# Sums of squares in the heads and around the embedding: high and low halves, multiplied with ones in the rounded format

## The chip, the cores and the metric

The kernel runs on one core of a Trainium2 chip. TensorE (PE) multiplies 128x128 tiles, VectorE (DVE), ScalarE (ACT) and GpSimd (POOL) work elementwise, and SyncE (SP) issues most of the DMAs. The metric is the device time of one execution in microseconds; a lower one is better.

## The reference

A sequence of 512 tokens of width 1024 goes through three layers in float32: a layer with differential attention, a short convolution and a gated embedding; a layer with a Fourier mixer and a SwiGLU; and a layer with four retention heads and a SwiGLU. What matters here are the root-mean-square norms:

```
attn = rms_norm(attn, subln_gain[i], SUBLN_EPS) * (1.0 - lambda_init)     # per attention head, 128 features
x = x + rms_norm(mixed, post_norm_gain[i])                                # "post", 1024 features
e = rms_norm(p[i] @ w_ple_proj[i], ple_norm_gain[i])                      # "ple", the embedding
x = x + jax.nn.sigmoid(x @ w_ple_gate[i]) * e
...
y = (y - mu) * lax.rsqrt(var + EPS)                                       # per retention head, 512 features
```

## The kernel before

Everything is held with features on the 128 partitions and tokens along the row (512), so the sum of squares over features of a norm crosses partitions. It is made in two steps. ACT squares the tiles of 128x512 and DVE adds them into `sqsum`; then PE multiplies `sqsum` with a 128x128 matrix of ones, which sums over partitions and spreads the result to all of them (`stats`, L1765). ACT takes logarithm and exponential of it (`rsqrt`, L439) and leaves `rinv`.

Weights stream from HBM in chunks of 8 tiles of 128x128 (512 KB). SP loads a chunk into `w_raw` (L325), ACT rounds it to `w_hi` in float32r (L430), POOL subtracts and leaves the rest in `w_lo` (L399, four pieces a chunk), and PE makes each product of three multiplications, `w_lo` with the rounded activations, `w_hi` with their rest, and `w_hi` with the rounded ones (`mul`, L1610: rows L1614, L1617, L1618). A group below means these three. Each buffer of a chunk comes free when PE has used it. The multiplications with ones alone are in plain float32: `ones` and `sqsum` are float32 tensors.

Each engine runs its instructions in the order in which the code writes them, and semaphores tie the engines together. The order around the norms:

- **Attention heads** (a loop of four turns; the last turn's tail runs in the gemm of `w_out`). PE multiplies the softmax weights with the values (`values`, L1836), then goes on with groups of the next gemm; after the tenth of them (`body_tail`, n == 9) it waits for `o_sq` and does `stats`, after the fifteenth (n == 14) it turns `ada_acc` with eight transposes (`ada_turn`, L1795). ACT copies and squares the attention output (L581, L582) and then copies the convolution output (L584), rounds a chunk and waits for the sum. DVE in between finishes the convolution (L1194) and does three steps of `ada` (L891, a chunk of ADA times a scalar, added to `ada_acc`): one, then the rest of the convolution output, then two. `ada_raw` has two buffers, so SP issues the load for one step when the step before last has run. After these steps DVE makes the head's output (L1207 on).
- **After the heads** ACT loads the embedding's input through its own queue (L593), rounds it (L595), and only then rounds the chunks of the `out` gemm from its fifth on.
- **"post"** (`norm_stats`, L1776). Seven of the eight squares are in `sqsum`; the eighth is multiplied with ones apart, from `sq`, and both products add up in the bank. It stands after tile m == 1 of the embedding's gemm (`gemm_e`). `rinv` then starts DVE's chain L1245, L1246, L1239, which makes X and its low part for the gate gemm, eight times.
- **"ple"** is the same in the gate gemm, after group n == 27. Its `rinv` starts DVE's chain of eight embedding tiles (L1263) and eight gate tiles (L1289, L1290, L1275, L1283), and its end lets PE form the next norm's columns (`rinv_columns`, L1939, row L1943).
- **Retention heads**. The squares of four tiles are added by DVE (`add_sq`, L1508); PE multiplies them after group n == 4 of the tile t + 10 (`group_stats`, L2102). Then come `product`, `normed`, `gate` and `y_low` on DVE, with ACT's `gate` and `y_high` between them. The last head's `y_low(3)` (L1531) is needed soon after by the gemm of `w_ret_out`.

Of the kernel before, what the change touches and what calls it, by code (L numbers as in the profile page):

```python
# [16 lines left out]
P = 128  # L17
# [122 lines left out]
def build(nc, W, ADA, XT, PT, COLS, DIST, ROPE, DECAY, OUT):  # L140
# [3 lines left out]
    with ctx:  # L144
# [25 lines left out]
        ones = sb("ones", [P, P])  # L170
# [82 lines left out]
        zc_t, cv_out = sem("zc_t"), sem("cv_out")  # L253
        p_hi, p_ready = sem("p_hi"), sem("p_ready")
# [35 lines left out]
        def added(v):  # L290

            return 6 * (v - (v > 3))
# [127 lines left out]
        def _(act):  # L420
# [136 lines left out]
            with act.Fori(0, NH) as i:  # L557
# [24 lines left out]
                act.activation(sqsum[:, :], banks[:, 4, :], ACT.Square).then_inc(o_sq, 1)  # L582
                act.wait_ge(cv_out, at("one", 1))
# [22 lines left out]

            def e_tile(m):
                t = TI["ple"] + m
                wait_tile(act, flat, t)
                read_out(act.activation(E[:, m, :], banks[:, BANK[t], :], ACT.Copy), t)  # L610
# [5 lines left out]
            e_tile(0)  # L616
            e_tile(1)
# [37 lines left out]
            for n in range(8):  # L655
                if n not in (3, 7):
                    split_w(flat, c0 + n + 4)
                if n == 1:
# [115 lines left out]
            def head(at, c, t):  # L774
# [44 lines left out]
                for n in range(3):  # L819
                    y_high(n)  # L820
# [47 lines left out]
        def _(dve):  # L868
# [47 lines left out]
            def add_square(v, m):  # L916

                if m in (-1, 0, KD - 1):
                    return
# [137 lines left out]
            dve.memset(ones[:, :], 1.0).then_inc(const, 1)  # L1057
# [86 lines left out]
            with dve.Fori(0, NH) as i:  # L1144
# [49 lines left out]
                dve.tensor_tensor(tmp[:, 0, :], tmp[:, 0, :], sq[:, 1, :], ALU.mult).then_inc(cv_out, 1)  # L1194
                ada(at, 1)
# [40 lines left out]

            def xg_lo(m):
# [15 lines left out]
            for m in range(KD):  # L1253
                add_square(2, m)

# [218 lines left out]
            def head(at, t):  # L1474
# [44 lines left out]
                add_sq(3)  # L1519

# [71 lines left out]
        def _(pe):  # L1592
# [43 lines left out]
            def split_tiles(v, t0, ks, rhs, ready, mid):  # L1636
# [15 lines left out]
                for m in SPLIT[v]:  # L1652
                    out = banks[:, BANK[t0 + m], BACK]
                    wait_bank(flat, t0 + m)
                    for n, k in enumerate(ks):
# [3 lines left out]
                        if count == mid:  # L1659
                            pe.wait_ge(half_sum, SPLIT_AT[v] + len(SPLIT[v]))  # L1660
                            pe.matmul(aux[:, FRONT], ones[:, :], sqsum[:, FRONT], start=True,
# [7 lines left out]
            def back_stats(v):  # L1669
                pe.wait_ge(full_sum, v - 3)  # L1670
                pe.wait_ge(half_ln, v - 3)
                pe.matmul(aux[:, BACK], ones[:, :], sqsum[:, BACK], start=True, stop=True).then_inc(aux_ready, 1)
# [92 lines left out]
            def stats(at, u):  # L1765
# [3 lines left out]
                pe.matmul(aux, ones[:, :], sqsum[:, :], start=True, stop=True).then_inc(aux_ready, 1)  # L1769

            def keep_warm(n=1):

                for _ in range(n):
                    pe.matmul(banks[:, 6, :], ones[:, :], cols[:, 0:S], start=True, stop=True)

            def norm_stats(v, name):  # L1776

                pe.wait_ge(sq_added, added(v) + 6)
                if AUX[name] > 0:
                    pe.wait_ge(aux_free, AUX[name])  # L1780
                pe.matmul(aux, ones[:, :], sqsum[:, :], start=True, stop=False)
                pe.wait_ge(sq_ready, 8 * v + 8)
                pe.matmul(aux, ones[:, :], sq[:, 1, :], start=False, stop=True).then_inc(aux_ready, 1)
                if name not in ("post", "ple", "final"):
                    keep_warm(2 if name == "four" else 1)
# [19 lines left out]
            for _ in range(WARM):  # L1805
                pe.matmul(banks[:, 6, 0:P], ones[:, :], ones[:, :], start=True, stop=True)
# [58 lines left out]
            def body_tail(at, n):  # L1865
# [49 lines left out]
            def gemm_e(t0):  # L1915

                for m in range(KD):
# [3 lines left out]
                    if m == 1:  # L1921
                        norm_stats(1, "post")
# [7 lines left out]
            def gate_hook(n):  # L1930
                if n == 27:
                    norm_stats(2, "ple")
# [169 lines left out]
            def group_stats(at):  # L2102

                pe.wait_ge(y_qs, at("three", 3))
                stats(at, AUX["ret"])
# [168 lines left out]
```

## Time and profile before

| | us |
|---|---|
| median of 3 runs | 1576.48 |
| lowest and highest of them | 1573.29, 1576.93 |
| the profiled execution | 1575.09 |
| its span | 1573.1 |
| PE busy in it | 1551.9 (99%) |
| DVE, ACT, POOL busy | 810.0, 594.5, 871.9 |

The span is the time between the first and the last instruction of the profiled execution, 2.0 us less than its own time. The granted clock of PE was full in all 40 slices of the span. A row of a timeline gives the start and the time taken in us, engine, line, operation and tiles, and, in brackets, how long the engine had been idle and what ended that. Ends of PE rows are modelled: the start of the next row tells what a multiplication took from its neighbours.

### The profile page before, as it was taken

To read this page: it belongs to the slowest core of one execution; us is meant where nothing else is said; L and a number is where in the kernel's file an instruction comes from. 1 tells how busy PE (TensorE), PEld (TensorE's weight loads), DVE (VectorE), ACT (ScalarE), POOL (GpSimd) and SP (SyncE) were. 2 spreads that over 40 slices of the span, in tenths; PEclk is the share of its full clock that TensorE was granted. 3 is DMA by queue.
4 is the path that set the end of the run, shared out by engine and by line. 5 is a ranking of instruction groups with operands and counts; after the bars stand their busy time and mean duration, and the time that the engine had idled before them with its cause. 6 is when DMAs were issued, how large, how long until landed. Compare 5 with 4: busy or idle time off the path is not lost.

```text
span 1573.1 us, 21372 instructions
## 1 busy us (share of the span) xinstructions
PE 1551.9 (99%) x7316; PEld 1286.8 (82%) x7316; DVE 810.0 (51%) x1131; ACT 594.5 (38%) x873; POOL 871.9 (55%) x1040
## 2 busy tenths in 40 slices
PE   8999999999999999999999999999999999999997
PEld 7777778898888888888888888888888888888886
DVE  6887786888744533542655424445258454012114
ACT  6434444674522212222444334244345322122224
POOL 6454448547576765675463644525534776555551
PEclk9999999999999999999999999999999999999999
DMA  6524455235255555542231322213212553333221
GB/s 215 201 96 163 181 197 191 79 124 173 69 200 200 177 204 183 184 174 94 93 120 56 115 82 79 93 53 105 93 54 67 201 188 133 95 100 100 93 80 54
DMA packets 58234, 202.99 MB, mean 129 GB/s; under 512 B 6464, under 2 KB 8512, under 8 KB 58176
## 3 DMA queue, kind: packets, MB, share of 16 engines
q1 hardware_dynamic: 56880, 198.87, 37.1%
q10 hardware_dynamic: 1296, 3.30, 0.6%
q8 instruction: 41, 0.67, 0.2%
q14 instruction: 17, 0.14, 0.0%
HBM read 200.05 MB, written 2.10 MB: 129 GB/s over the span
## 4 chain that ended last, share of the span: by engine, by line
PE 72%; issue 12%; POOL 12%; DVE 2%; ACT 1%; DMA 1%; SPq 0%; POOLq 0%; DVEq 0%; ACTq 0%
PE banks L1614 20%; PE banks L1618 20%; PE banks L1617 20%; POOL w_lo L399 12%; PE banks L2097 2%; PE banks L2094 2%; PE banks L2098 2%; PE banks L2132 1%; PE banks L2133 1%; PE banks L2134 1%; PE banks L1630 1%; PE banks L1634 1%; PE banks L1633 1%; PE banks L1801 0%; PE banks L2120 0%
## 5 line engine op out<-in xcount | busy, mean ns | idle before, releaser
L399 POOL TENSOR_TENSOR w_lo<-w_raw,w_hi 128x256 fp32r<-128x256 f32 x1032 | 868.3, 874 | 666.3 <-ACT w_hi L430 666.1
L430 ACT ACTIVATE w_hi<-w_raw 128x1024 fp32r<-128x1024 f32 x258 | 271.3, 1057 | 658.5 <-PE banks L1614 596.4
L1614 PE MATMUL banks<-a_hi,w_lo 128*128 128x512 f32 x1228 | 485.0, 395 | 0.0
L1618 PE MATMUL banks<-a_hi,w_hi 128*128 128x512 f32 x1228 | 478.2, 389 | 0.0
L1617 PE MATMUL banks<-a_lo,w_hi 128*128 128x512 f32 x1228 | 477.9, 389 | 0.0
L1614 PEld LDWEIGHTS banks<-a_hi,w_lo 128*128 128x128 f32 x1228 | 230.7, 188 | 48.7 <-issue 2.2
L1618 PEld LDWEIGHTS banks<-a_hi,w_hi 128*128 128x128 f32 x1228 | 230.5, 188 | 48.7
L1617 PEld LDWEIGHTS banks<-a_lo,w_hi 128*128 128x128 f32 x1228 | 230.7, 188 | 48.5 <-issue 2.2
L1614 PE MATMUL banks<-b_hi,w_lo 128*128 128x512 f32 x572 | 223.8, 391 | 0.0
L1618 PE MATMUL banks<-b_hi,w_hi 128*128 128x512 f32 x572 | 222.6, 389 | 0.0
L1617 PE MATMUL banks<-b_lo,w_hi 128*128 128x512 f32 x572 | 222.5, 389 | 0.0
L891 DVE SCALAR_TENSOR_TENSOR ada_acc<-ada_raw,small,ada_acc 128x1024 f32<-128x1024 f32 x98 | 154.6, 1577 | 44.0 <-DMA ada_raw<-in_ADA 41.7
L1036 DVE SCALAR_TENSOR_TENSOR X<-banks,mod,X 128x512 f32<-128x512 f32 x64 | 47.0, 747 | 155.6 <-PE banks L1618 155.4
L1614 PEld LDWEIGHTS banks<-b_hi,w_lo 128*128 128x128 f32 x572 | 107.4, 188 | 22.7 <-issue 0.6
L1617 PEld LDWEIGHTS banks<-b_lo,w_hi 128*128 128x128 f32 x572 | 107.4, 188 | 22.6 <-issue 0.5
L1618 PEld LDWEIGHTS banks<-b_hi,w_hi 128*128 128x128 f32 x572 | 107.4, 188 | 22.4
L1370 DVE TENSOR_TENSOR scr<-scr,banks 128x512 f32<-128x512 f32 x44 | 30.3, 688 | 96.1 <-PE banks L1618 95.1
L1366 DVE SCALAR_TENSOR_TENSOR scr<-scr,banks 128x512 f32<-128x512 f32 x44 | 30.2, 687 | 94.2 <-ACT scr L721 94.2
L1378 DVE SCALAR_TENSOR_TENSOR b_lo<-scr,b_hi 128x512 f32 (+1 forms) x44 | 34.1, 775 | 50.6 <-ACT b_hi L728 50.6
L2094 PE MATMUL banks<-w_lo,a_hi 128*128 128x512 f32 x128 | 49.8, 389 | 0.0
L2097 PE MATMUL banks<-w_hi,a_lo 128*128 128x512 f32 x128 | 49.8, 389 | 0.0
L2098 PE MATMUL banks<-w_hi,a_hi 128*128 128x512 f32 x128 | 49.8, 389 | 0.0
(255 smaller groups left out, 1675.5 us busy)
## 6 DMA issues: line engine op xcount, KB each, us to landing
w_raw<-in_W SPq DMA_DIRECT2D x258, 512.0 KB, 3.5
ada_raw<-in_ADA SPq DMA_DIRECT2D x112, 512.0 KB, 4.2
X<-in_XT SPq DMA_DIRECT2D x8, 256.0 KB, 6.9
scr<-in_DECAY ACTq DMA_DIRECT2D x4, 448.0 KB, 3.3
out<-X SPq DMA_DIRECT2D x2, 512.0 KB, 3.0
out<-X SPq DMA_DIRECT2D x3, 256.0 KB, 3.0
w_raw<-in_W SPq DMA_DIRECT2D x2, 256.0 KB, 3.8
scr<-in_PT ACTq DMA_DIRECT2D x1, 512.0 KB, 5.1
```

What stands on the lines that cost most here:

```text
L399: pool.tensor_tensor(w_lo[:, c % RING, part], w_raw[:, c % RING, part], w_hi[:, c % RING, part].bitcast(fp32), ALU.subtract).then_inc(wlo, 1)
L430: act.activation(w_hi[:, c % RING, :], w_raw[:, c % RING, :], ACT.Copy).then_inc(whi, 1)
L891: ins = dve.scalar_tensor_tensor(out=ada_acc[:, :], in0=src, scalar=cact[:, f:f + 1], in1=ada_acc[:, :], op0=ALU.mult, op1=ALU.add)
L1036: read_out(dve.scalar_tensor_tensor(out=X[:, m, :], in0=banks[:, BANK[t], :], scalar=mod[:, KD * g + m:KD * g + m + 1], in1=X[:, m, :], op ...
L1370: read_out(dve.tensor_tensor(HD[:, n, :], SG[:, n, :], banks[:, BANK[u], :], ALU.mult), u)
L1378: dve.scalar_tensor_tensor(out=lo, in0=HD[:, n, :], scalar=0.5, in1=hi.bitcast(fp32), op0=ALU.mult, op1=ALU.subtract).then_inc(hid_ready, 1)
L1614: mm = pe.matmul(out, lo, x_hi, start=first, stop=False)
L1617: pe.matmul(out, hi, x_lo, start=False, stop=False)
L1618: mm = pe.matmul(out, hi, x_hi, start=False, stop=last)
L2094: mm = pe.matmul(out, a_hi[:, k, c], wl, start=(k == 0), stop=False)
L2097: pe.matmul(out, a_lo[:, k, c], wh, start=False, stop=False)
L2098: mm = pe.matmul(out, a_hi[:, k, c], wh, start=False, stop=(k == KD - 1))
```

## The change

- In the heads (attention and retention) and for "post" and "ple", ACT copies `sqsum`, complete, into a free slot of `b_hi` in the rounded format, and DVE subtracts that from `sqsum` into the same slot of `b_lo`. PE multiplies both with `ones_r` and adds them in the bank (`sum_of`), instead of the float32 multiplication.
- For "post" and "ple" DVE also adds the eighth square; PE no longer takes it from `sq`.
- Four places move. In `gemm_e` the sum comes after m == 2 instead of m == 1, in the gate gemm after n == 30 instead of 27, in the retention heads after n == 6 instead of 4. In the retention heads `split_w(at, c + 6)` moves behind two `y_high`, and `y_low(0)` before `product(2)`.
- `ones` becomes a float32 view of `ones_r`, which DVE fills by way of `tmp` at the start. The first norm, the norms that are cut in front and back halves, and the columns keep the float32 form.

```diff
+        ones_r = sb("ones_r", [P, P], f32r)
+        ones = ones_r[:, :].bitcast(fp32)
...
-            return 6 * (v - (v > 3))
+            return (0, 6, 13, 20, 20, 26, 32, 38)[v]
...
                 act.activation(sqsum[:, :], banks[:, 4, :], ACT.Square).then_inc(o_sq, 1)
+                act.wait_ge(o_sq, at("one", 1))
+                act.activation(b_hi[:, 8, :], sqsum[:, :], ACT.Copy).then_inc(o_sum, 1)
...
+            def sum_high(n, v):
+                act.wait_ge(sq_added, added(v) + 7)
+                act.activation(b_hi[:, 10, :], sqsum[:, :], ACT.Copy).then_inc(sum_hi, 1)
...
             e_tile(0)
+            sum_high(0, 1)
             e_tile(1)
...
+                if n == 0:
+                    sum_high(1, 2)
...
+                act.wait_ge(y_qs, at("three", 3))
+                act.activation(b_hi[:, 4, :], sqsum[:, :], ACT.Copy).then_inc(y_sum, 1)
                 rsqrt(AUX["ret"], 4 * P, eps6, y_r, at)
                 gate(2, t + 10)
-                split_w(at, c + 6)
...
-                for n in range(3):
-                    y_high(n)
+                y_high(0)
+                y_high(1)
+                split_w(at, c + 6)
+                y_high(2)
...
-                if m in (-1, 0, KD - 1):
+                if m in (-1, 0) or (v, m) == (0, KD - 1):
...
-            dve.memset(ones[:, :], 1.0).then_inc(const, 1)
+            link(dve.memset(tmp[:, 0, 0:P], 1.0))
+            dve.tensor_scalar(ones_r[:, :], tmp[:, 0, 0:P], 1.0, None, ALU.mult).then_inc(const, 1)
...
                 dve.tensor_tensor(tmp[:, 0, :], tmp[:, 0, :], sq[:, 1, :], ALU.mult).then_inc(cv_out, 1)
+                dve.wait_ge(o_sum, at("one", 1))
+                dve.tensor_tensor(b_lo[:, 8, :], sqsum[:, :], b_hi[:, 8, :].bitcast(fp32), ALU.subtract).then_inc(o_rest, 1)
                 ada(at, 1)
...
+            def sum_low(n):
+                dve.wait_ge(sum_hi, n + 1)
+                dve.tensor_tensor(b_lo[:, 10, :], sqsum[:, :], b_hi[:, 10, :].bitcast(fp32),
+                                  ALU.subtract).then_inc(sum_lo, 1)
...
                 add_sq(3)
+                dve.wait_ge(y_sum, at("one", 1))
+                dve.tensor_tensor(b_lo[:, 4, :], sqsum[:, :], b_hi[:, 4, :].bitcast(fp32), ALU.subtract).then_inc(y_rest, 1)
...
                 gate(at, 2, t + 10)
+                y_low(0)
                 product(2, t + 10)
                 normed(2)
-                for n in range(3):
+                for n in range(1, 3):
                     y_low(n)
...
+            def sum_of(slot):
+
+                pe.matmul(aux, ones_r[:, :], b_lo[:, slot, :], start=True, stop=False)
+                pe.matmul(aux, ones_r[:, :], b_hi[:, slot, :], start=False, stop=True).then_inc(aux_ready, 1)
...
                 if n == 9:
-                    pe.wait_ge(o_sq, at("one", 1))
-                    stats(at, A0 + 5)
+                    pe.wait_ge(o_rest, at("one", 1))
+                    pe.wait_ge(aux_free, at("aux", A0 + 5))
+                    sum_of(8)
...
-                    if m == 1:
-                        norm_stats(1, "post")
+                    if m == 2:
+                        norm_stats(0, "post")
...
-                if n == 27:
-                    norm_stats(2, "ple")
+                if n == 30:
+                    norm_stats(1, "ple")
...
-                gemm(at, t + 10, 1, range(KD), rhs_a, None, False, lambda n: group_stats(at) if n == 4 else None)
+                gemm(at, t + 10, 1, range(KD), rhs_a, None, False, lambda n: group_stats(at) if n == 6 else None)
```

On DVE, in the loop of the attention heads, at the end of the convolution, the order before is this (`tmp<-tmp,sq` is the last product of the convolution, `ada_acc` the steps of `ada`):

```order
L891 SCALAR_TENSOR_TENSOR ada_acc<-ada_raw,small,ada_acc 128x1024
L1191 SCALAR_TENSOR_TENSOR sq<-tmp,banks 128x512
L1194 TENSOR_TENSOR tmp<-tmp,sq 128x512
L891 SCALAR_TENSOR_TENSOR ada_acc<-ada_raw,small,ada_acc 128x1024
L1198 SCALAR_TENSOR_TENSOR b_lo<-tmp,b_hi 128x512
L891 SCALAR_TENSOR_TENSOR ada_acc<-ada_raw,small,ada_acc 128x1024 x2
L1207 TENSOR_TENSOR tmp<-sq,rinv 128x512
```

and after the change, where its line numbers are 15 to 18 higher, this:

```order
L906 SCALAR_TENSOR_TENSOR ada_acc<-ada_raw,small,ada_acc 128x1024
L1207 SCALAR_TENSOR_TENSOR sq<-tmp,banks 128x512
L1210 TENSOR_TENSOR tmp<-tmp,sq 128x512
L1212 TENSOR_TENSOR b_lo<-sqsum,b_hi 128x512
L906 SCALAR_TENSOR_TENSOR ada_acc<-ada_raw,small,ada_acc 128x1024
L1216 SCALAR_TENSOR_TENSOR b_lo<-tmp,b_hi 128x512
L906 SCALAR_TENSOR_TENSOR ada_acc<-ada_raw,small,ada_acc 128x1024 x2
L1225 TENSOR_TENSOR tmp<-sq,rinv 128x512
```

The subtraction L1212 stands, with its wait for ACT, ahead of the last three steps of `ada` and of the head's output.

On ACT, from the end of the `out` gemm to the "post" norm, the order before is (`scr<-banks` are the embedding's tiles):

```order
L437 ACTIVATE sq<-banks 128x512
L610 ACTIVATE scr<-banks 128x512 x2
L441 ACT_TABLE_LOAD
L443 ACTIVATE rinv<-banks,small 128x512
L445 ACTIVATE rinv<-rinv 128x512
```

and after the change:

```order
L440 ACTIVATE sq<-banks 128x512
L619 ACTIVATE scr<-banks 128x512
L614 ACTIVATE b_hi<-sqsum 128x512
L619 ACTIVATE scr<-banks 128x512
L444 ACT_TABLE_LOAD
L446 ACTIVATE rinv<-banks,small 128x512
L448 ACTIVATE rinv<-rinv 128x512
```

The copy L614, which waits for DVE's last addition, stands ahead of the second embedding tile and of the table load.

## Rows read from the trace of the kernel before

**Rows 1.** The page, busy us, share of the span and instructions of each engine.

```profile
PE 1551.9 (99%) x7316; PEld 1286.8 (82%) x7316; DVE 810.0 (51%) x1131; ACT 594.5 (38%) x873; POOL 871.9 (55%) x1040
```

**Rows 2.** Waits of PE, the longest: who waited for whom, us in total, times, longest one.

```profile
PE banks L1661 <- DVE sqsum L959: 3.0, 2, 1.8
```

**Rows 3.** Groups of PE by line and shape: count, busy us, mean ns, idle.

```profile
L1769 PE MATMUL banks<-sqsum,ones 128*128 128x512 f32 x18 | 9.3, 597 | 1.2 <-DVE sqsum L1079 1.2
```

**Rows 4.** Timeline of DVE in the second attention head.

```profile
119.07 0.69 DVE L1194 TENSOR_TENSOR tmp<-tmp,sq 128x512 f32<-128x512 f32 x1
119.68 1.28 DVE L891 SCALAR_TENSOR_TENSOR ada_acc<-ada_raw,small,ada_acc 128x1024 f32<-128x1024 f32 x1
...
122.17 1.28 DVE L891 SCALAR_TENSOR_TENSOR ada_acc<-ada_raw,small,ada_acc 128x1024 f32<-128x1024 f32 x1 [0.61 <-DMA ada_raw<-in_ADA]
125.38 1.28 DVE L891 SCALAR_TENSOR_TENSOR ada_acc<-ada_raw,small,ada_acc 128x1024 f32<-128x1024 f32 x1 [1.93 <-DMA ada_raw<-in_ADA]
```

**Rows 5.** The same stretch, ACT: the square that the sum is made of.

```profile
119.35 0.59 ACT L582 ACTIVATE sqsum<-banks 128x512 f32<-128x512 f32 x1
```

**Rows 6.** The same stretch, SP's queue: two issues of `ada` loads.

```profile
118.61 0.33 SPq L331 DMA_DIRECT2D ada_raw<-in_ADA  x1
...
121.12 0.33 SPq L331 DMA_DIRECT2D ada_raw<-in_ADA  x1
```

**Rows 7.** Timeline of PE: second head, `out` gemm, "post", "ple", dft, last retention head.

```profile
123.50 1.02 PE L1769 MATMUL banks<-sqsum,ones 128*128 128x512 f32 x2
...
124.58 0.39 PE L1617 MATMUL banks<-a_lo,w_hi 128*128 128x512 f32 x1
...
127.81 1.03 PE L1801 MATMUL banks<-cols,ada_acc 128*128 128x128 f32 x8
...
240.68 0.39 PE L1614 MATMUL banks<-b_hi,w_lo 128*128 128x512 f32 x1
...
246.12 0.41 PE L1614 MATMUL banks<-b_hi,w_lo 128*128 128x512 f32 x1
...
270.64 1.02 PE L1781 MATMUL banks<-sqsum,ones 128*128 128x512 f32 x2
...
272.59 0.39 PE L1617 MATMUL banks<-b_lo,w_hi 128*128 128x512 f32 x1
...
335.61 0.95 PE L1943 MATMUL banks<-ones,sqsum 128*128 128x1 f32 x8
...
1178.29 0.39 PE L1614 MATMUL banks<-b_hi,w_lo 128*128 128x512 f32 x1
```

**Rows 8.** Timeline of POOL: the four pieces of the `out` gemm's fifth chunk.

```profile
241.55 4.36 POOL L399 TENSOR_TENSOR w_lo<-w_raw,w_hi 128x256 fp32r<-128x256 f32 x4 [10.27 <-ACT w_hi L430]
```

**Rows 9.** The page, DMA issues: line, queue, count, KB each, median us to landing.

```profile
ada_raw<-in_ADA SPq DMA_DIRECT2D x112, 512.0 KB, 4.2
...
scr<-in_PT ACTq DMA_DIRECT2D x1, 512.0 KB, 5.1
```

**Rows 10.** Timeline of ACT: last square and logarithm of "post", logarithm of "ple".

```profile
269.38 0.58 ACT L437 ACTIVATE sq<-banks 128x512 f32<-128x512 f32 x1
...
272.75 0.69 ACT L443 ACTIVATE rinv<-banks,small 128x512 f32<-128x512 f32 x1
...
303.37 0.69 ACT L443 ACTIVATE rinv<-banks,small 128x512 f32<-128x512 f32 x1
```

**Rows 11.** Timeline of DVE: chain after "post", chain after "ple", last retention head.

```profile
279.66 0.69 DVE L1239 TENSOR_TENSOR a_lo<-X,a_hi 128x512 fp32r<-128x512 f32 x1 [0.58 <-ACT a_hi L614]
...
281.99 0.97 DVE L1239 TENSOR_TENSOR a_lo<-X,a_hi 128x512 fp32r<-128x512 f32 x1 [0.17 <-ACT a_hi L614]
...
305.25 9.21 DVE L1263 SCALAR_TENSOR_TENSOR scr<-scr,small,rinv 128x512 f32<-128x512 f32 x8
...
334.57 0.68 DVE L1283 TENSOR_TENSOR sqsum<-sqsum,banks 128x512 f32<-128x512 f32 x1
...
1176.91 0.69 DVE L1531 SCALAR_TENSOR_TENSOR b_lo<-scr,b_hi 128x512 fp32r<-128x512 f32 x1 [0.70 <-ACT b_hi L817]
```

More of the change, by code:

```diff
@@ L169, in build @@
         cols = sb("cols", [P, NCOL])
-        ones = sb("ones", [P, P])
+        ones_r = sb("ones_r", [P, P], f32r)
+        ones = ones_r[:, :].bitcast(fp32)
         small = sb("small", [P, 72])
@@ L253, in build @@
         zc_t, cv_out = sem("zc_t"), sem("cv_out")
+        o_sum, o_rest, y_sum, y_rest = (sem(n) for n in ("o_sum", "o_rest", "y_sum", "y_rest"))
+        sum_hi, sum_lo = sem("sum_hi"), sem("sum_lo")
         p_hi, p_ready = sem("p_hi"), sem("p_ready")
@@ L1235, in _ @@
             t1 = TI["ple"]
+            def sum_low(n):
+                dve.wait_ge(sum_hi, n + 1)
+                dve.tensor_tensor(b_lo[:, 10, :], sqsum[:, :], b_hi[:, 10, :].bitcast(fp32),
+                                  ALU.subtract).then_inc(sum_lo, 1)
+            sum_low(0)
             def xg_lo(m):
@@ L1254, in _ @@
                 add_square(2, m)
+            sum_low(1)
             t0 = TI["gate"]
@@ L1660, in split_tiles @@
                             pe.wait_ge(half_sum, SPLIT_AT[v] + len(SPLIT[v]))
-                            pe.matmul(aux[:, FRONT], ones[:, :], sqsum[:, FRONT], start=True,
+                            pe.matmul(aux[:, FRONT], ones, sqsum[:, FRONT], start=True,
                                       stop=True).then_inc(half_stats, 1)
@@ L1671, in back_stats @@
                 pe.wait_ge(half_ln, v - 3)
-                pe.matmul(aux[:, BACK], ones[:, :], sqsum[:, BACK], start=True, stop=True).then_inc(aux_ready, 1)
+                pe.matmul(aux[:, BACK], ones, sqsum[:, BACK], start=True, stop=True).then_inc(aux_ready, 1)
             def split_start(t0, a, v, rhs):
@@ L1768, in stats, with norm_stats @@
                     pe.wait_ge(aux_free, at("aux", u))
[L1769 to L1785, printed above, removed]
+                pe.matmul(aux, ones, sqsum[:, :], start=True, stop=True).then_inc(aux_ready, 1)
+            def sum_of(slot):
+                pe.matmul(aux, ones_r[:, :], b_lo[:, slot, :], start=True, stop=False)
+                pe.matmul(aux, ones_r[:, :], b_hi[:, slot, :], start=False, stop=True).then_inc(aux_ready, 1)
+            def norm_stats(n, name):
+                pe.wait_ge(sum_lo, n + 1)
+                pe.wait_ge(aux_free, AUX[name])
+                sum_of(10)
             def ada_columns(at, u, g):
@@ L1805, in _ @@
             for _ in range(WARM):
-                pe.matmul(banks[:, 6, 0:P], ones[:, :], ones[:, :], start=True, stop=True)
+                pe.matmul(banks[:, 6, 0:P], ones, ones, start=True, stop=True)
             A0, t0 = AUX["body"], TI["body"]
@@ L2102, in group_stats @@
             def group_stats(at):
-                pe.wait_ge(y_qs, at("three", 3))
-                stats(at, AUX["ret"])
+                pe.wait_ge(y_rest, at("one", 1))
+                pe.wait_ge(aux_free, at("aux", AUX["ret"]))
+                sum_of(4)
             def head(at, t):
```

## The prediction, made before the changed kernel had run

> **What bounds the kernel now.** I read the page first, its busy shares, then the waits of PE, then the timelines around each place that the diff touches. PE is busy 1551.9 us, 99% of the span [rows 1]. No other engine comes near, and the longest entry in the list of PE's waits is 3.0 us in two waits at a norm that isn't touched [rows 2]. So PE's own work sets the time, and what PE is spared counts, as long as nothing else becomes late. The list of waits tells who did hold PE up, not who was about to. That second thing decides this case, and it is in the timelines: how early each operand was ready when PE came for it.
>
> **What PE is spared.** From the first row of the "post" sum to the second multiplication of the next group are 272.59 - 270.64 = 1.95 us, for two float32 multiplications of 128x512 and one in the rounded format [rows 7]. A rounded one takes 0.227 us: 24 of them fill the chunk from 240.68 to 246.12, 5.44 us [rows 7]. That leaves 1.72 us for two float32 ones, 0.86 us each. The sum in the second head agrees: 124.58 - 123.50 = 1.08, less 0.23, is 0.85 us [rows 7]. The trace shows each as two rows: 18 rows of L1769 are nine sums, the first norm and eight heads [rows 3]. So a head's sum falls from 0.86 to 2 x 0.227 = 0.45 us, a saving of 0.41, eight times 3.3 us. "post" and "ple" fall from 1.72 to 0.45, a saving of 1.27 each, 2.5 us. Together PE has 5.8 us less to do. The few hundredths at the start for filling `ones_r` I take as nothing: PE's warm-up multiplications are followed by a wait for POOL anyway; bounds are 0 and one DVE operation of 0.3 us.
>
> **Attention heads.** What is added is one ACT copy and one DVE subtraction, and their place on DVE is what costs. ACT's square begins at 119.35 and takes 0.59 [rows 5]; a copy of the same shape another 0.6; DVE's subtraction, like L1194, 0.69 [rows 4]; two hand-overs of about 0.1 us are an estimate. DVE is through at about 121.4. PE wants the sum at 123.50 [rows 7], so the sum itself is in time. But DVE began a step of `ada` at 119.68 [rows 4], and now begins it at 121.4, 1.7 us later. Queued behind it are the load of the step after next, that step, and the head's output. SP issued that load at 121.12 [rows 6], when the step had ended, and DVE began on its data at 125.38, having idled 1.93 us for it [rows 4]. Now the issue is at 122.8. From issue to use took 4.26 us here and 3.56 us for the load before (118.61 to 122.17) [rows 4, 6]. The new load starts when fewer bytes are under way, so I take 3.9, between the two. The step then begins at 126.7 and ends at 128.0, 1.3 us later than before. PE turns `ada_acc` and was there at 127.81 [rows 7]; spared 0.41 us, it comes at 127.4 and waits 0.7 us for the data (with a hand-over of 0.1). A head thus costs PE 0.3 us more than before instead of 0.41 less; with 3.56 and 4.26 for the load it is -0.05 and +0.65. Four heads are alike: +1.2 us (-0.2 to +2.6).
>
> After the fourth head the lateness goes one step further. DVE's output, ACT's copy of it, the embedding's load in ACT's queue behind that copy, its rounding, and the `out` gemm's fifth chunk stand in one row, all 1.3 us later. POOL finished that chunk at 241.55 + 4.36 = 245.91 [rows 8], and PE began it at 246.12 [rows 7]: 0.2 us to spare. Now it is ready at 247.2, while PE would come at 246.4. That is another +0.8, whatever the load takes. Heads together: **+2.0 us** (+0.6 to +3.4).
>
> **"post", "ple" and the gates.** Here PE's 2.5 us are spared inside a stretch whose end a DVE chain sets. The last square of "post" ends at 269.38 + 0.58 [rows 10]. To it come an addition on DVE after the copy of the tile (to 271.3), ACT's copy (to 272.0) and DVE's subtraction (to 272.7). PE, moved one tile later, is there at 270.64 + 1.36 = 272.0 and waits 0.8 us. ACT's table load stands behind its copy, so the logarithm, at 272.75 before [rows 10], comes at about 273.75: +1.0. DVE's chain after it had idle time, 0.58 and 0.17 us before L1239 [rows 11] among it, that takes up 0.75; 0.25 remains. At "ple" an addition and ACT's copy stand ahead of the logarithm. The addition is covered by a chunk's rounding on ACT, the copy isn't: +0.6 on 303.37 [rows 10]. Its `rinv` is thus 0.85 late. From the eight rows that begin at 305.25 to L1283 at 334.57 DVE has no gap to catch up [rows 11]. It ended at 334.57 + 0.68 = 335.25, and PE, which needs that sum, came at 335.61 [rows 7]: 0.36 us to spare. Now DVE ends at 336.1. PE would come at 335.61 - 2.5 + 0.8 = 333.9 and waits 2.2 us. So nothing of the 2.5 us is left, and PE leaves at +0.5. Four more DVE operations read two operands from SBUF, partly beside POOL. L1239 took 0.69 us at 279.66 and 0.97 at 281.99, with POOL at work [rows 11]; four times 0.28 is 1.1 us at most, and I add 0.3. The stretch costs **+0.8 us** (+0.2 to +1.8).
>
> The Trainium skill, page "SBUF — State Buffer", section "Who interferes with whom", says that the port pair that VectorE shares with GpSimd is locked for a whole instruction, and the loser blocks fully. By that rule each of the four would wait up to a whole piece of POOL's and the stretch would stand at its upper bound, 1.0 us above my value. The two rows of L1239 show a prolongation of 0.28 us, not of a piece; I stay with the rows.
>
> **Retention heads.** Two groups later, PE comes 1.36 us after the old place. ACT's copy waits for the last addition and falls behind a rounding that was there before; the subtraction is done about 0.5 us before PE comes. Nothing waits for `ada` here. `rinv` is 1.36 - 0.41 = 0.95 later. `product` and `normed` move by as much, and `y_low(0)` now fills a wait for the gate. In three heads the outputs are needed only after the 32 groups of the next gemm, 22 us. In the last, `y_low(3)` ended at 1176.91 + 0.69 = 1177.60 [rows 11] and PE wanted it at 1178.29 [rows 7]. About half of the lateness is taken up by idle time, 0.70 us before that row among it: it ends at 1178.1, and PE comes at 1177.9. Four times -0.41, and a wait of 0.2 (0 to 1.0): **-1.4 us** (-1.65 to -0.6).
>
> **The sum.** 2.0 + 0.8 - 1.4 = +1.4 us on the profiled execution's own 1575.09 us, span 1573.1 and 2.0 around it: **1576.5 us**. The bounds add up to -0.85 and +4.6. The profiled execution lies 1.4 us below the median of 1576.48 and between the two outer runs; I keep to it, and leave the scatter of the runs to the range.
>
> **Rivals.** (1) All of it reaches the end. PE is the busiest engine by far, and the moves of the sums look like room for the new steps. Then 5.8 us go: 1569.3. Against it stand the two ends with 0.2 and 0.36 us to spare. Chance 0.07. (2) The heads' loads land so early that PE meets no wait at the turn: a load quicker than 3.5 us, and then a chunk that is on time. The heads give -1.65, the rest stays: -1.65 + 0.8 - 1.4 = -2.2, 1572.9. For it speaks the load of 3.56; against it that the spare time at the turn was 1.15 us and the step is 1.7 late. Chance 0.15. (3) Slower: the moved `ada` load meets the load of the next chunk and takes 5.1 us, as the embedding's load of the same size did [rows 9], 1.2 above my 3.9. Each head then costs +1.5, four 6.0, and with the chunk's 0.8: 6.8 + 0.8 - 1.4 = +6.2, 1581.3. It decides from a load of about 4.7 us on; the median of all is 4.2 [rows 9]. Chance 0.08. The forecast has 0.70.
>
> **How the numbers follow.** A measurement of this kernel can tell some 0.3%, 4.7 us, from no change. Rival 1 alone is faster by more: 0.07. Rival 3 and the forecast's upper edge are slower by more: 0.09. The rest, 0.84, is no change. The range runs from 1572.0, which takes in rival 2, to 1580.5, the forecast's upper bound of 1579.7 with some scatter of the runs; rivals 1 and 3 stay out.
>
> **What would show it.** In the changed kernel's waits of PE there should be four waits at the transposes of `ada_acc` for DVE's step, about 0.7 us each; one of 0.8 at the `out` gemm's fifth chunk for POOL; one of 0.8 at the "post" sum; about 2.2 us in one or more before `rinv_columns`, for DVE's additions or its low parts; and a short one for the last `y_low`. PE's busy time should fall by some 5.8 us while the span stays. Rows of the new sums should start 0.227 us apart. It is wrong if the turns show no wait, or if PE reaches `rinv_columns` without one; and above all if the rounded sums take longer than 0.45 us.

## The result, and the profile after

The changed kernel takes 1579.92 us (median of 12 runs, 1577.62 to 1583.71), the kernel before 1576.19 us beside it (12 runs, 1573.29 to 1578.00). The ratio is 1.0027, 95% interval 1.0019 to 1.0035. That is 3.7 us in the medians: inside the 0.3% that I called no change, but a loss. The forecast was 1576.5, a loss of 1.4 on its own execution.

First the page, then the waits of PE (columns as in [rows 2]).

```profile
PE 1554.3 (98%) x7312; PEld 1290.5 (82%) x7312; DVE 818.3 (52%) x1144; ACT 599.2 (38%) x883; POOL 879.0 (56%) x1040
...
scr<-in_PT ACTq DMA_DIRECT2D x1, 512.0 KB, 6.2
```

```profile
PE banks L1798 <- DVE sqsum L1095: 2.9, 1, 2.9
...
PE banks L1802 <- DVE b_lo L1257: 1.8, 1, 1.8
PE banks L1690 <- DVE sqsum L974: 1.8, 1, 1.8
PE banks L1643 <- POOL w_lo L402: 1.7, 1, 1.7
...
PE banks L1825 <- DVE ada_acc L906: 1.2, 4, 0.3
...
PE banks L1997 <- DVE a_lo L1331: 0.4, 1, 0.4
PE banks L1997 <- DVE b_lo L1301: 0.3, 1, 0.3
...
PE banks L1968 <- DVE sqsum L1309: 0.3, 1, 0.3
PE banks L1997 <- DVE sqsum L1309: 0.2, 1, 0.2
```

Three kinds of waits are new: the "post" sum waits 1.8 us (L1802), the `out` gemm's fifth chunk 1.7 us for POOL (L1643), the four turns of `ada_acc` 0.3 each (L1825). The last four rows, 1.2 us together, lie around `rinv_columns` (L1968); the 0.4 for `a_lo` among them stood in the kernel before too (0.4 there), so 0.8 are new. The longest row, 2.9 us, is the first norm's sum, which the change leaves in float32. It waited 1.2 us in the kernel before [rows 3] and 2.6 in before_early, a kernel below whose only edit lies at 234 us, so it is scatter of the executions. By the first turn (74.87 us before, 76.59 after) the two traces are 1.7 us apart, by this wait and the clock around it. PE should be less busy, but the page says 2.4 us more than [rows 1]. The clock is why: in the kernel heads_later, below, which makes the same sums and was traced at a mean clock of 0.997, PE was busy 1547.1 us, 4.8 less than before. The stretches of both kernels in which it differed, the kernel after first: PE's busy time and rows, the other engines, the granted clock, the DMA share and GB/s.

```profile
20.00:30.00 10.00, 7.09 (x23) 4.75 (x22) 5.97 (x12) 5.28 (x7) 3.86 (x5) 0.83 0.61 209
...
279.00:290.00 11.00, 11.00 (x37) 9.31 (x36) 6.87 (x11) 4.77 (x9) 0.98 (x2) 0.53 0.18 66
...
1198.00:1206.00 8.00, 6.22 (x38) 5.96 (x37) 6.35 (x17) 3.64 (x9) 0.00 (x0) 0.79 0.02 7
```

```profile
20.00:30.00 10.00, 8.79 (x38) 6.61 (x37) 6.63 (x13) 6.20 (x8) 3.83 (x5) 1.00 0.64 205
...
279.00:290.00 11.00, 11.00 (x50) 9.12 (x49) 10.13 (x13) 6.40 (x11) 7.38 (x8) 1.00 0.16 48
```

In the second of them PE is busy all 11 us in both kernels, but does 37 rows instead of 50: 1.2 GHz for most of the stretch instead of 2.4. So this one execution, at 1583.71 us the slowest of the twelve, must not be subtracted from that of before, which ran at full clock up to 1566 us and at half for its last 6 us, when PE's work is all but done, as every traced kernel does at its end. Every run lists its mean granted clock, and that separates the two causes:

| kernel | mean clock of its runs | runs at a clock of 0.995 | their median |
|---|---|---|---|
| before (104 runs) | 0.9955 | 29 | 1577.0 |
| after (12 runs) | 0.9948 | 8 | 1580.1 |

At the same clock the loss is 3.1 us; the rest comes with 0.0007 of clock. A straight line through all 256 runs, with a level for each kernel and one slope for all, gives 1.27 us for each 0.001 of clock (±0.14), and the kernel after stands 3.0 us (±0.9) above the kernel before. I use that figure, called "at equal clock", for the experiments too.

Where the 3 us come from is in the timelines. First DVE in the second head (L1212 is the new subtraction):

```profile
120.85 0.69 DVE L1210 TENSOR_TENSOR tmp<-tmp,sq 128x512 f32<-128x512 f32 x1
122.45 0.69 DVE L1212 TENSOR_TENSOR b_lo<-sqsum,b_hi 128x512 fp32r<-128x512 f32 x1 [0.90 <-ACT b_hi L587]
123.06 1.28 DVE L906 SCALAR_TENSOR_TENSOR ada_acc<-ada_raw,small,ada_acc 128x1024 f32<-128x1024 f32 x1
124.25 1.23 DVE L1216 SCALAR_TENSOR_TENSOR b_lo<-tmp,b_hi 128x512 f32 x1
125.40 1.76 DVE L906 SCALAR_TENSOR_TENSOR ada_acc<-ada_raw,small,ada_acc 128x1024 f32<-128x1024 f32 x1
128.03 1.50 DVE L906 SCALAR_TENSOR_TENSOR ada_acc<-ada_raw,small,ada_acc 128x1024 f32<-128x1024 f32 x1 [0.87 <-DMA ada_raw<-in_ADA]
```

The same head on SP's queue, POOL and PE: the load that the step at 128.03 uses, the chunk, the sum and the turn.

```profile
124.50 0.33 SPq L334 DMA_DIRECT2D ada_raw<-in_ADA  x1
```

```profile
123.97 4.49 POOL L402 TENSOR_TENSOR w_lo<-w_raw,w_hi 128x256 fp32r<-128x256 f32 x4 [8.07 <-ACT w_hi L433]
```

```profile
125.28 0.40 PE L1802 MATMUL banks<-b_lo,ones_r 128*128 128x512 f32 x1
125.52 0.39 PE L1803 MATMUL banks<-b_hi,ones_r 128*128 128x512 f32 x1
125.75 0.39 PE L1643 MATMUL banks<-a_hi,w_lo 128*128 128x512 f32 x1
...
129.67 1.09 PE L1825 MATMUL banks<-cols,ada_acc 128*128 128x128 f32 x8 [0.33 <-DVE ada_acc L906]
```

The sum takes 125.75 - 125.28 = 0.47 us, as forecast. From its start to the turn PE takes 129.67 - 125.28 = 4.39 us, against 127.81 - 123.50 = 4.31 before [rows 7]: the wait takes back all that the sum saves. The load was used 128.03 - 124.50 = 3.53 us after its issue. L1216 and the step behind it run beside POOL now and take 1.23 and 1.76 us. Before, such a step took 1.28 there [rows 4]; for L1216 the kernel heads_later, below, has the other value.

Then the fifth chunk, on ACT, POOL and PE:

```profile
237.35 0.34 ACTq L598 DMA_DIRECT2D scr<-in_PT  x1
243.59 1.06 ACT L600 ACTIVATE b_hi<-scr 128x1024 fp32r<-128x1024 f32 x1 [5.77 <-DMA scr<-in_PT]
```

```profile
245.68 4.33 POOL L402 TENSOR_TENSOR w_lo<-w_raw,w_hi 128x256 fp32r<-128x256 f32 x4 [11.09 <-ACT w_hi L433]
```

```profile
250.15 0.47 PE L1643 MATMUL banks<-b_hi,w_lo 128*128 128x512 f32 x1 [1.73 <-POOL w_lo L402]
```

And the "post" sum, on DVE, ACT and PE:

```profile
273.34 1.65 DVE L906 SCALAR_TENSOR_TENSOR ada_acc<-ada_raw,small,ada_acc 128x1024 f32<-128x1024 f32 x1 [0.73 <-DMA ada_raw<-in_ADA]
274.91 0.68 DVE L1249 COPY scr<-banks 128x512 f32<-128x512 f32 x1
275.51 0.68 DVE L938 TENSOR_TENSOR sqsum<-sqsum,sq 128x512 f32<-128x512 f32 x1
276.89 1.12 DVE L1257 TENSOR_TENSOR b_lo<-sqsum,b_hi 128x512 fp32r<-128x512 f32 x1 [0.70 <-ACT b_hi L614]
```

```profile
273.47 0.58 ACT L440 ACTIVATE sq<-banks 128x512 f32<-128x512 f32 x1
...
276.22 0.63 ACT L614 ACTIVATE b_hi<-sqsum 128x512 fp32r<-128x512 f32 x1 [1.69 <-DVE sqsum L938]
```

```profile
278.06 0.50 PE L1802 MATMUL banks<-b_lo,ones_r 128*128 128x512 f32 x1 [1.80 <-DVE b_lo L1257]
```

The last square ends at 274.05, but a step of `ada` stands on DVE until 274.99, so that the last addition ends at 276.19, 2.1 us behind the square.

### The profile page after: what moved, and what is told of

It reads as the page before. It is cut to its first block, busy times and chain, and to the rows that moved or that the text cites. A ratio compares the mean times of both kernels' runs of the same rounds, so it can differ in the third digit from the quotient of the medians.

```text
span 1581.5 us, 21395 instructions
## 1 busy us (share of the span) xinstructions
PE 1554.3 (98%) x7312; PEld 1290.5 (82%) x7312; DVE 818.3 (52%) x1144; ACT 599.2 (38%) x883; POOL 879.0 (56%) x1040
## 4 chain that ended last, share of the span: by engine, by line
PE 79%; issue 9%; POOL 7%; DVE 3%; ACT 2%; DMA 1%; SPq 0%; POOLq 0%; DVEq 0%; ACTq 0%
PE banks L1643 21%; PE banks L1646 21%; PE banks L1647 21%; POOL w_lo L402 7%; PE banks L2122 2%; PE banks L2119 2%; PE banks L2123 2%; PE banks L1659 1%; PE banks L1662 1%; PE banks L1663 1%; PE banks L2158 1%; PE banks L2160 1%; PE banks L2159 1%; DVE scr L1289 1%; PE banks L1825 0%
## 5 line engine op out<-in xcount | busy, mean ns | idle before, releaser
L1643 PE MATMUL banks<-a_hi,w_lo 128*128 128x512 f32 x1228 | 482.3, 393 | 0.0
L1643 PEld LDWEIGHTS banks<-a_hi,w_lo 128*128 128x128 f32 x1228 | 231.1, 188 | 47.6 <-issue 0.5
L1643 PE MATMUL banks<-b_hi,w_lo 128*128 128x512 f32 x572 | 224.4, 392 | 1.7 <-POOL w_lo L402 1.7
L1643 PEld LDWEIGHTS banks<-b_hi,w_lo 128*128 128x128 f32 x572 | 108.1, 189 | 24.9 <-issue 2.1
```

The source lines that it names most:

```text
L1643: mm = pe.matmul(out, lo, x_hi, start=first, stop=False)
```

## Experiments

Twelve kernels, each timed beside the kernel before, whose median was 1575.89 us next to the first three and fill_waits, 1575.40 next to heads_later, best1, post_only and ple_only, and 1575.83 next to the last four. The ratio is against the runs of the same group, and is not the quotient of the two medians. "At equal clock" is the distance to the kernel before by the line above, ±0.9 for each.

| kernel | median | ratio, 95% interval | mean clock | at equal clock |
|---|---|---|---|---|
| ret_only | 1573.86 | 0.9993 (0.9982 to 1.0003) | 0.9959 | -1.4 |
| heads_only | 1578.26 | 1.0015 (1.0005 to 1.0024) | 0.9952 | +2.1 |
| norms_only | 1578.03 | 1.0015 (1.0002 to 1.0028) | 0.9951 | +1.6 |
| post_only | 1578.12 | 1.0020 (1.0008 to 1.0031) | 0.9943 | +1.1 |
| ple_only | 1578.09 | 1.0011 (1.0000 to 1.0022) | 0.9945 | +0.3 |
| fill_waits | 1578.34 | 1.0023 (1.0008 to 1.0038) | 0.9950 | +2.8 |
| heads_later | 1576.14 | 1.0004 (0.9994 to 1.0014) | 0.9953 | -0.2 |
| best1 | 1574.23 | 0.9988 (0.9979 to 0.9997) | 0.9959 | -1.7 |
| before_early | 1575.53 | 0.9997 (0.9988 to 1.0006) | 0.9957 | -0.3 |
| after_early | 1576.76 | 1.0002 (0.9992 to 1.0013) | 0.9952 | +0.2 |
| all_early | 1574.84 | 0.9988 (0.9978 to 0.9998) | 0.9950 | -1.9 |
| best2 | 1573.82 | 0.9978 (0.9967 to 0.9988) | 0.9956 | -2.7 |

**The parts alone.** Each takes the new sums in one place and the old ones, in their old place, everywhere else. Of the changed kernel, ret_only for one takes back this in the attention heads, with the copy and the subtraction that feed it, and puts `norm_stats` of before, after m == 1 and n == 27, in the place of the new one:

```diff
-                    pe.wait_ge(o_rest, at("one", 1))
-                    pe.wait_ge(aux_free, at("aux", A0 + 5))
-                    sum_of(8)
+                    pe.wait_ge(o_sq, at("one", 1))
+                    stats(at, A0 + 5)
...
-                    if m == 2:
-                        norm_stats(0, "post")
+                    if m == 1:
+                        norm_old(1, "post")
```


ret_only: 

> The kernel before, with the rounded sums of the four retention heads alone, y_low(0) and the chunk moved as in the change. All theories: 4 x 0.41 less and a short wait for the last low part, -1.3 to -1.6 us, 1574.6 to 1575, with full clock; the profile's first stretch, up to 790 us, stays as before. If the clock of other places sets the times, the difference drowns in it.

heads_only: 

> The kernel before, with the rounded sum in the four attention heads alone. By the shifts between the two profiles: per head the sum gives 0.41 us and the wait at the turn takes 0.45 back, and the fifth chunk is 2.0 us later. Theory A (waits and a clock drop after a long one): +2.3 us from waits, and up to 2 us more where the clock falls after the chunk's wait of 1.7 us, 1578 to 1580.5. Theory B (waits alone): +2.3 us, 1578 to 1579. My prediction's sum had +2.0. Rival C (the heads cost nothing, the whole loss is at the embedding): -1.6 us, 1574.6.

norms_only: 

> The kernel before, with the rounded sums of post and ple alone. The ada loads of the out gemm stay on time here, so PE should wait 0.8 us at the post sum, as the prediction had it, and not 1.8. Theory A (a wait lowers the clock only when it is long): no half clock after it, and +0.5 to +1.0 us from the DVE chains that end at the dft's columns, less what the next norm's wait gives back (1.3 us in the changed kernel): 1575.5 to 1577. Theory A' (any wait there lowers the clock): +3 to +5 us, 1579 to 1581. Rival C (the embedding's sums alone bring the loss): the same 1579 to 1581, with full clock.

The retention heads gain 1.4 us, the attention heads lose 2.1, the two norms 1.6. The sum is +2.3, against 3.0 for the whole. So the parts add up within their errors, and the loss has two seats. ret_only came as said. heads_only has the +2.3 of theory B, and rival C falls. norms_only lies above theory A's +0.5 to +1.0 (+1.6, and +2.4 by its ratio) and below the +3 of the other two. In the traced execution of heads_only the waits of PE name them:

```profile
PE banks L1632 <- POOL w_lo L402: 1.8, 1, 1.8
...
PE banks L1822 <- DVE ada_acc L900: 1.2, 4, 0.3
```

That is the fifth chunk and the four turns. The turns' 0.3 only eats the 0.4 that the sum saves. Starts of PE's rows show it without the scatter of whole executions: from the first turn to the fourth, three heads, PE took 158.80 us in the kernel before, 159.14 in the changed one and 159.18 in heads_only, at full clock in all three. So a head costs 0.1 us, and nearly all of the heads' loss is at the chunk.

**post_only and ple_only** cut the norms in two. post_only: 

> The post norm's sum alone in halves, all others in float32. With the ple norm it lost 2.1 us. Theory A (each norm loses by its own wait): post saves 1.3 of TensorE's time and waits 1.1, so it stands within 0.5 us of the kernel before, and the 2 us belong to the ple norm or to the half clock. Theory B (post loses them): its wait and the later ends of ScalarE and VectorE behind it cost 1.5 to 2.5 us, and the ple norm costs nothing.

ple_only: 

> The ple norm's sum alone in halves. The counterpart of the run before: theory A (each norm within 0.5 us of the kernel before, as long as `rinv_columns` waits less than 1 us) against theory B (by the prediction the later root holds `rinv_columns` and costs 0.5 us or more: +0.5 to +2).

+1.1 and +0.3 make 1.4, near the 1.6 of both, and point at "post", whose wait is 1.2 us in its trace; post_only falls between its two theories. With ±0.9 on each that is no proof, and the medians alone, 1578.12 and 1578.09, don't tell them apart. The trace of post_only also waits 1.1 us at the fifth chunk, behind an embedding load of 6.5 us, though its heads are those of the kernel before. So a part of its loss is the chunk's and not the norm's.

**fill_waits** asks whether the waits cost clock beyond themselves. Ahead of two waits of PE it puts seven rounded multiplications each, whose result is overwritten:

```diff
+                    for _ in range(7):
+                        pe.matmul(aux, ones_r[:, :], b_hi[:, 0, :], start=True, stop=True)
...
-                pe.wait_ge(sum_lo, n + 1)
                 pe.wait_ge(aux_free, AUX[name])
+                for _ in range(7 if name == "post" else 0):
+                    pe.matmul(aux, ones_r[:, :], b_hi[:, 8, :], start=True, stop=True)
+                pe.wait_ge(sum_lo, n + 1)
```

> The changed kernel, with seven rounded multiplications of 128x512 (7 x 0.227 = 1.6 us, their result is overwritten) put into PE's order at each of its two long waits: ahead of the out gemm's fifth chunk, where it waited 1.7 us for POOL, and ahead of the post sum, where it waited 1.8 us for DVE. The waits' ends stay where they are. Theory A (the waits lower the granted clock: in the changed kernel's profile it stood at half for 10 us right after the post wait, and PE's rows took 0.43 instead of 0.23 us there): the drop goes away, about 3.5 to 5 us less than the changed kernel, within 0.1% of the kernel before, 1574 to 1577 us, and the profile shows full clock from 280 to 290 us. Theory B (the time is lost in the waits and in the DVE chains alone): no change against the changed kernel, 1579.5 to 1580.5 us, ratio to before 1.0025 to 1.003.

The traced execution kept the full clock up to 1564 us, as theory A wants it, and took 1575.98 us, 7.7 less than the changed kernel's traced one. On that pair alone the clock would be the whole story. Twelve runs say otherwise: the mean clock is 0.9950 against 0.9948, and at equal clock the kernel stands at +2.8 against +3.0. The median of 1578.34 lies between the two theories, and theory A's gain of 3.5 to 5 us did not come. A smaller one is not excluded: with twelve runs on each side the difference of the mean clocks is known to ±0.0011, and the added multiplications themselves take time when the chunk is ready early (in this trace the embedding's load took 5.1 us, in the changed kernel's 6.2). Half-clock stretches also stand where the change did nothing: before_early, whose only edit lies at 234 us, has one between 20 and 30 us.

```profile
20.00:30.00 10.00, 7.40 (x24) 5.27 (x23) 5.80 (x12) 6.22 (x9) 3.69 (x5) 0.83 0.63 210
```

The clock of a single execution is thus scatter of a few us, on top of what the change does. But the scatter is not all. The eight kernels with a new "post" or "ple" sum have a mean clock of 0.9949 (94 runs), the six without one 0.9956 (162 runs), a difference of 0.0007 ± 0.0003. And the traces show a place: in five of those eight PE runs at half clock for about 3.4 us between 342 and 351 us, right behind `rinv_columns` and its waits, in none of the other six. In norms_only (columns as above, stretches of 2 us):

```profile
344.00:346.00 2.00, 2.00 (x31) 2.00 (x32) 0.78 (x2) 0.00 (x0) 0.00 (x0) 1.00 0.35 133
346.00:348.00 2.00, 2.00 (x14) 2.00 (x15) 0.00 (x0) 1.98 (x4) 0.84 (x2) 0.77 0.00 0
348.00:350.00 2.00, 2.00 (x12) 2.00 (x11) 1.91 (x5) 2.00 (x5) 1.96 (x3) 0.50 0.00 0
```

So "at equal clock" leaves out a part of what the new norm sums cost, some 0.9 us by the line above (0.7 times 1.27). That the waits at `rinv_columns` bring it about is not shown; fill_waits did not fill those.

**heads_later** moves one instruction of the changed kernel, with its wait:

```diff
-                dve.wait_ge(o_sum, at("one", 1))
-                dve.tensor_tensor(b_lo[:, 8, :], sqsum[:, :], b_hi[:, 8, :].bitcast(fp32), ALU.subtract).then_inc(o_rest, 1)
                 ada(at, 1)
+                dve.wait_ge(o_sum, at("one", 1))
+                dve.tensor_tensor(b_lo[:, 8, :], sqsum[:, :], b_hi[:, 8, :].bitcast(fp32), ALU.subtract).then_inc(o_rest, 1)
```

> The changed kernel, with one edit: in the heads VectorE's subtraction for the sum stands behind the step of `ada` that it stood ahead of. Same work in every other respect. Theory A (the subtraction's place costs): the step of `ada` runs as early as before the change, its load is issued as early, the four turns wait 0.1 us or less for `ada_acc` (0.3 each in the changed kernel), TensorE waits less than 0.5 us for GpSimd's halves at the fifth chunk (1.7 in the changed kernel), and the post sum's wait falls from 1.8 to about 1; median 3 to 4 us less than the changed kernel's: about 1576. Theory B (the new sums themselves bring the loss, by TensorE's pauses at the norms and at half clock): the waits at the turns go, yet the median stays within 1.5 us of the changed kernel's, 1578.5 to 1581.

Theory A holds: 3.6 us less by the ratios, 3.2 at equal clock (3.0 by the medians against their groups), from the order of two DVE instructions. From the first turn to the fourth PE now takes 157.58 us, 0.5 less for each head than in the changed kernel and 0.4 less than in the kernel before: there the saving comes in full. It is level with the kernel before. The turns are gone from the waits of PE, the "post" wait is 1.2. DVE in the same head:

```profile
118.49 1.28 DVE L906 SCALAR_TENSOR_TENSOR ada_acc<-ada_raw,small,ada_acc 128x1024 f32<-128x1024 f32 x1
119.68 0.69 DVE L1213 TENSOR_TENSOR b_lo<-sqsum,b_hi 128x512 fp32r<-128x512 f32 x1
120.29 0.69 DVE L1216 SCALAR_TENSOR_TENSOR b_lo<-tmp,b_hi 128x512 f32 x1
121.42 1.36 DVE L906 SCALAR_TENSOR_TENSOR ada_acc<-ada_raw,small,ada_acc 128x1024 f32<-128x1024 f32 x1 [0.45 <-DMA ada_raw<-in_ADA]
```

The subtraction no longer idles 0.90 us for ACT's copy; the step of `ada` covers it. And L1216 is clear of POOL: it takes 0.69 us again. In its groups by shape, first here and then in the changed kernel, the four of L1216 are:

```profile
L1216 DVE SCALAR_TENSOR_TENSOR b_lo<-tmp,b_hi 128x512 f32 x4 | 2.7, 684 | 0.0
```

```profile
L1216 DVE SCALAR_TENSOR_TENSOR b_lo<-tmp,b_hi 128x512 f32 x4 | 4.9, 1229 | 0.0
```

The Trainium skill, page "SBUF — State Buffer", section "Who interferes with whom", says that a VectorE instruction with two inputs in SBUF contends with a GpSimd instruction that reads SBUF. L1216 is such a one, and the trace agrees: 1229 ns beside POOL, 684 without.

The expected wait below 0.5 us at the fifth chunk did not come: it is 0.9. The embedding's load is the reason. It took 5.1 us in the kernel before [rows 9], 6.2 in the changed one, 6.3 in heads_only, 5.7 here.

**best1** is heads_later's heads with ret_only's retention and the old norms. 

> Sums in halves in the heads, with the subtraction behind the step of `ada`, and in the retention; the post and ple norms in their old form. Theory A: the heads give their four times 0.4 us in full, and the retention the 2.0 that it gave alone: 3 to 3.7 us less than the kernel before, about 1572.5. Theory B: the heads' saving is lost behind the last chunks of the out gemm, whose loads end last whatever stands on VectorE: what the retention gave alone is all, -2.0, about 1574.

Theory B: 0.9988, which is -1.9 us, a median of 1574.23, and -1.7 at equal clock. From the first turn to the fourth its traced execution takes 157.59 us, so the heads give their 0.4 each; then PE waits 1.9 us for the fifth chunk, with a load of 6.6 us. What PE is spared in the heads meets that load.

**The fifth chunk ahead of the embedding.** ACT waits for the embedding's load with the chunks' rounding behind it, though the fifth chunk's data is there. One edit turns the two around:

```diff
             act.dma_start(PV, PT).then_inc(p_in, 16)
+            c0, t0 = CH["out"], TI["out"]
+            split_w(flat, c0 + 4)
             act.wait_ge(p_in, 16)
             act.activation(b_hi[:, 8:10, :].rearrange("p k s -> p (k s)"), PV, ACT.Copy).then_inc(p_hi, 1)
-            c0, t0 = CH["out"], TI["out"]
             for n in range(8):
-                if n != 3:
+                if n not in (0, 3):
```

before_early: 

> The kernel before with one edit: ScalarE makes the high half of the out gemm's fifth chunk (`split_w`) ahead of its wait for the embedding's load, not behind it. In the kernel before TensorE hardly waits at that chunk, so both theories expect next to nothing: -0.3 to 0.3 us. If it gains more than 0.5, the edit does something of its own, and the three kernels beside it have to be read against this one.

after_early: 

> The changed kernel with that edit. Theory A (the heads' saving is lost at the fifth chunk, since ScalarE stands behind the embedding's load): the wait for GpSimd there, 1.7 us in the changed kernel, goes, and the kernel is 2.0 us faster than the changed one: ratio to the kernel before about 1.0015. Theory B (the heads lose at the turns, and the next wait takes what the chunk gives back): within 0.5 us of the changed kernel, ratio 1.0025 to 1.003.

all_early: 

> The changed kernel with both edits: the heads' subtraction behind the step of `ada`, and the fifth chunk's high half ahead of the embedding's load. Theory A: 1.0 us below the kernel with the first edit alone, whose traced run waits 0.9 us at the fifth chunk: ratio to the kernel before 0.9995 to 1. Theory B (the post sum waits for VectorE's chain, which no chunk moves): nothing, ratio 1.0004.

best2: 

> Heads (subtraction behind the step of `ada`) and retention in halves, post and ple in float32, and the fifth chunk's high half ahead of the embedding's load. Without the last edit this kernel waits 1.9 us at the fifth chunk. Theory A: that wait goes in full, and with four times 0.4 of the heads and 1.65 of the retention the kernel is 3 to 3.5 us below the kernel before: ratio 0.998. Theory B (given back at the next wait): what it was without, ratio 0.999.

ACT and POOL in the traced execution of all_early:

```profile
234.88 0.34 ACTq L598 DMA_DIRECT2D scr<-in_PT  x1
235.33 1.06 ACT L433 ACTIVATE w_hi<-w_raw 128x1024 fp32r<-128x1024 f32 x1
240.58 1.06 ACT L602 ACTIVATE b_hi<-scr 128x1024 fp32r<-128x1024 f32 x1 [4.19 <-DMA scr<-in_PT]
```

```profile
236.47 2.83 POOL L402 TENSOR_TENSOR w_lo<-w_raw,w_hi 128x256 fp32r<-128x256 f32 x4 [3.21 <-ACT w_hi L433]
```

The chunk is ready at 239.30, not at 245.91 as in [rows 8]. In all four kernels that is 4.4 us after the load's issue, against 11.6 before, with loads of 4.9 to 5.7 us, and in none of them does PE wait for it. before_early gains nothing that can be told (-0.3). after_early stands at +0.2 against the changed kernel's +3.0, so the chunk was worth 2.8 us there (±1.1), with a traced wait of 1.7. all_early, the change with both edits, is 1.9 us below the kernel before by its ratio (0.9988, and as much at equal clock); heads_later alone was at 1.0004. best2, which keeps the float32 sums at "post" and "ple", reaches 0.9978 (0.9967 to 0.9988): 3.5 us faster than the kernel before by its ratio, 2.7 at equal clock, 2.0 in the medians. It beats both kernels. Theory A held each time in kind. In size two expectations were too small: after_early's ratio was to be 1.0015 and its interval ends at 1.0013 (at equal clock it lost 2.8 of the 3.0 where 2.0 had been said), and all_early gained 1.7 on heads_later at equal clock where 1.0 had been said. Both differences are within the errors of the equal-clock figures.

## Why the prediction was right or wrong, point by point

- **The sums.** Right. A sum takes 0.47 us where 0.45 was said, which is 0.2 us over all ten. The retention heads, whose cover was sound, gained 1.4 us as forecast (ret_only, ±0.8). The last `y_low` held up a weight load of PE by 0.4 us, and PE itself shows no wait there.
- **The heads, +2.0.** The total was right (+2.1 in heads_only), its division wrong, so the total is in part luck: the four heads took about 0.7 us less than said at their turns, the chunk 1 us more. The chain on DVE was read well. Counted from the convolution's last product, the step of `ada` begins 2.21 us later (123.06 - 120.85), against 0.61 before: 1.6 where 1.7 was said, and the 0.90 us for which the subtraction idles for ACT's copy are in that reckoning. The load was set at 3.9 us and took 3.53, the lower bound, and the turns waited 0.3 us instead of 0.7. A head then costs PE 0.1 us net, not 0.3. One thing was left out: L1216 and the step of `ada` behind it slid beside POOL.
- **The fifth chunk, +0.8.** The mis-sized term. "Whatever the load takes" was the wrong phrase. The lateness was reckoned with the embedding's load as in [rows 9]. Its issue moved as forecast: 1.62 us after the start of the fourth turn, against 0.65 before, that is 1.0 us later in relation to PE, as the forecast's 1.3 and 0.3 have it. But the load took 6.2 instead of 5.1, and PE waited 1.7. The row had a count of 1, and one execution showed one value of something that lies between 4.7 and 6.6 us over the fourteen traced kernels.
- **"post", +0.8 for the stretch.** Right in sign and chain, too small: +1.6 in norms_only, though ±0.9 reaches 0.8. PE waited 1.8 us at the "post" sum where 0.8 was said (1.1 and 1.2 in norms_only and post_only). The chain of copy, addition, copy, subtraction was taken to start from the last square. A step of `ada`, late with its loads, stood ahead of it on DVE. The subtraction took 1.12 us beside POOL where L1239 gave 0.97 as the longest [rows 11]. By the rule of the Trainium skill's page "SBUF — State Buffer" the stretch would have stood 1.0 us higher, at 1.8. The 1.6 of norms_only is nearer to that than to my 0.8, but the rows don't bear the rule's size out: this subtraction was prolonged by 0.43 us, where one of POOL's pieces of 128x256 took about 1.1 (4.33 us for four). And in its section "Who interferes with whom" the page says it of VectorE's 2-port modes; of instructions with two inputs in SBUF, as these are, it says that they contend.
- **`rinv_columns`, 2.2 us of waits.** Right in place, much smaller: 0.8 in three new waits in the changed kernel. The clock that falls right behind them, in five of eight traced kernels, was not foreseen.
- **The clock.** Not in the sum at all. The profiled execution of before had a clock of 0.998, and 4 runs of 104 had that; at 0.995, the clock of 29 of them, it takes 1577.0. The forecast was made on a rare execution, and the rows that were to be checked against the profile after met one on the other side, 0.992. "PE's busy time should fall by 5.8" failed for this reason: it rose by 2.4.
- **The time.** 1579.9 lies in the range, below its upper end by 0.6. Of the 3.4 us between forecast and median, about 1.1 is the profiled execution's distance to its own median (1575.09 to 1576.19). At equal clock 1.6 us are missing from the sum. The chunk and the "post" wait each came out about 1 us over their terms, the turns and `rinv_columns` under theirs.
- **The rivals.** The first fell: nothing like 5.8 us came through in any kernel. The second wanted a load quicker than 3.5 us, no wait at the turns and a chunk on time. The load took 3.53, the turns still waited 0.3 us each, and the chunk was late. In heads_later the turns are free, and its trace still waits 0.9 us at the chunk and 1.2 at "post". The third fell with its load of 5.1 us.

## What to carry to other kernels

A step that is added to a side engine costs by what is queued behind it. Put it behind the instruction that issues or frees the next load, when its consumer has time: here the order of two VectorE instructions was worth 3 us of 1576, more than the change saves on sums in the attention heads, four times 0.41. When the busiest engine is spared work, look at each load with a count of 1 that the next stage waits for, and take its landing time as a spread; an engine that waits for such a load should first do what is already there. And before two traces are subtracted, compare their granted clocks, and compare PE's starts between two marks inside them: that showed 0.1 us a head where whole executions scatter by several.

## What the runs showed of the hardware

- The same 512 KB load of the embedding, on ScalarE's queue, took 4.7 to 6.6 us from issue to landing in fourteen traced kernels.
- A VectorE instruction that reads two operands from SBUF took 1229 ns beside GpSimd's subtraction and 684 ns without it, in all four heads alike.
- One and the same kernel runs at different mean clocks: the kernel before had 0.993 to 0.998 in 104 runs. 0.001 of it goes with 1.27 us. In every traced kernel PE's clock is at half in the last 6 to 10 us of the execution, when PE's work is all but done.
